# Two projection blocks placed later in a hand-written order, and the experts' down weights read in one run for each partition

## The reference, cut to what matters

```
h = rmsnorm(x, g_attn);  proj = h @ w_in          # u | q_lat | kv_lat | k_pe | q_mem | 3 gates
c_kv = rmsnorm(kv_lat, g_kvlat)
q = rmsnorm(rmsnorm(q_lat, g_qlat) @ w_uq, g_qn)  # then rotary positions
k, v = keys_values(c_kv @ w_ukv)                  # norm and rotary positions on k
merged = sum_i sigmoid(gate_i) * branch_i         # A: S5, B: MLA, C: memory attention
x = x + merged @ w_out
h = rmsnorm(x, g_ffn)
for e in range(32):                               # 2 experts are chosen for each token
    hid = silu(h @ w_e1[e]) * (h @ w_e3[e])       # 1024 -> 256, two products
    y = y + gate[..., e:e+1] * (hid @ w_e2[e])    # 256 -> 1024
x = x + y
```

## Time and profile before

| | |
|---|---|
| median of 3 runs | 638.8 us (636.69, 638.80, 639.08) |
| the profiled execution's own time | 638.72 us |
| its span, first to last instruction | 636.9 us |
| granted TensorE clock, mean of full speed | 0.992 |
| PE busy | 606.7 us, 95% of the span |
| DVE, ACT, POOL busy | 50%, 29%, 23% |
| moved by DMA | 150.57 MB |
| largest shares of the chain that ended last | PE 89%, DVE 4%, issue 2%, DMA 2% |

### The profile page before, as it was taken

One profiled execution on the slowest core, in us unless ns is written; L12 is line 12 of the kernel. 1 busy time (PEld: TensorE's weight loads), 2 busy tenths in 40 slices (PEclk: granted clock), 3 DMA queues, 4 the chain that ended last, 5 costly groups with the idle time before them and its releaser, 6 DMA issues.

```text
span 636.9 us, 10034 instructions
## 1 busy us (share of the span) xinstructions
PE 606.7 (95%) x3742; PEld 378.3 (59%) x3742; DVE 321.1 (50%) x858; ACT 184.0 (29%) x579; POOL 149.1 (23%) x341
## 2 busy tenths in 40 slices
PE   8999999999999999999999999999999999887994
PEld 7888867777456667666677767854434443333441
DVE  3343947757883589772043222685524425425133
ACT  5534224532478445432100101212121121210100
POOL 1596627733584524510000000000000000000000
PEclk9999999999899999999999999999999999999899
DMA  9783553212301343323589990199999999999993
GB/s 302 180 289 108 193 171 100 68 66 84 113 2 33 127 139 100 100 67 100 150 255 395 404 388 20 38 369 415 417 416 415 418 415 417 418 416 418 412 408 112
DMA packets 61683, 150.57 MB, mean 236 GB/s; under 512 B 12352, under 2 KB 40448, under 8 KB 53696
## 3 DMA queue, kind: packets, MB, share of 16 engines
q1 hardware_dynamic: 61632, 149.89, 63.5%
HBM read 147.12 MB, written 2.76 MB: 235 GB/s over the span
## 4 chain that ended last, share of the span: by engine, by line
PE 89%; DVE 4%; issue 2%; DMA 2%; ACT 1%; SPq 0%; DVEq 0%
PE PS L832 28%; PE PS L842 21%; PE PS L1216 9%; PE PS L1113 7%; PE PS L1255 5%; PE PS L1245 5%; PE PS L958 2%; PE PS L915 2%; DVE X L2117 2%; PE PS L983 2%; PE PS L825 1%; PE PS L1166 1%; PE PS L1025 1%; DMA W<-in_w_in 1%; PE PS L966 1%
## 5 line engine op out<-in xcount | busy, mean ns | idle before, releaser
L832 PE MATMUL PS<-hT,W 128*128 128x320 f32 x416 | 117.2, 436 | 0.0
L832 PEld LDWEIGHTS PS<-hT,W 128*128 128x128 f32 x416 | 77.5, 190 | 33.4 <-issue 3.8
L1216 PE MATMUL PS<-E,xT 128*32 128x256 f32 (+1 forms) x1088 | 60.1, 374 | 8.5 <-issue 8.1
L1216 PEld LDWEIGHTS PS<-E,xT 128*32 128x32 f32 x1088 | 37.5, 112 | 35.5 <-issue 20.2
L2191 POOL TENSOR_SCALAR means<-sums 128x4 f32<-128x4 f32 (+3 forms) x35 | 7.6, 217 | 188.0 <-ACT junk L1358 187.1
L1113 PE MATMUL PS<-h,S 128*128 128x512 f32 (+1 forms) x96 | 48.2, 625 | 0.7 <-DVE S L1974 0.7
L1255 PE MATMUL PS<-yb,WG 128*128 128x512 f32 (+1 forms) x96 | 40.9, 622 | 4.0 <-DVE X L2117 3.1
L842 PE MATMUL PS<-W,hT 128*128 128x256 f32 (+5 forms) x256 | 41.7, 353 | 0.0
L2117 DVE TENSOR_TENSOR X<-X,PS 128x512 f32<-128x512 f32 (+1 forms) x48 | 32.8, 686 | 8.3 <-PE PS L1255 6.7
L842 PEld LDWEIGHTS PS<-W,hT 128*128 128x128 f32 (+1 forms) x256 | 31.5, 163 | 8.4 <-issue 1.3
L842 PE MATMUL PS<-W,mergedT 128*128 128x384 f32 (+3 forms) x192 | 35.7, 381 | 0.0
(11 more groups left out here) (313 smaller groups left out, 976.9 us busy)
## 6 DMA issues: line engine op xcount, KB each, us to landing
E<-in_w_e SPq DMA_DIRECT2D x93, 1024.0 KB, 21.3
W<-in_w_in SPq DMA_DIRECT2D x7, 1536.0 KB, 7.2
W<-in_w_in SPq DMA_DIRECT2D x7, 1024.0 KB, 8.6
W<-in_w_mem_kv SPq DMA_DIRECT2D x4, 1024.0 KB, 6.2
W<-in_w_glu SPq DMA_DIRECT2D x4, 768.0 KB, 7.7
W<-in_w_out SPq DMA_DIRECT2D x2, 1536.0 KB, 15.6
X<-in_x_prompt SPq DMA_DIRECT2D x4, 512.0 KB, 4.6
W<-in_w_o_mem SPq DMA_DIRECT2D x1, 1536.0 KB, 6.6
```

Of the source, the lines that this page charges most:

```text
L832: ins = mm(out[:, 0:TOK], w[:, k, cols:cols + 128], rhs[:, k, :], start=(k == 0), stop=(k == kt - 1))
L1216: ins = mm(PS[r:r + B, 2 + par, 128 * which.start:128 * which.stop], xT[:, k, place_ + B * n:place_ + B * n + B], E13[slot][:, which, k, 1 ...
```

## The change

Two edits, independent of each other. In `middle()`, the last `gateC` step (`gateC` 7) is put in after the `qlT` and `ckT` steps in place of before them, and the last `outC` step (`outC` 7) after `kqT` 15 in place of before it. The source of the down weights is viewed with two neighbouring rows of `w_e2` in one partition (`(p j)` for `(j p)`), so each partition reads 8 KB in one run. For the products to fit, half j of the up products takes every second column of the weights (`j::2`) and no longer 128 columns in a row.

```
-    fill(KD)
-    fills = [("outC", d) for d in range(KD)]
+    while len(fills) > 1:
+        fill()
     for t in range(NT):
         put("qlT", t)
     for j in range(len(KEYS)):
         put("ckT", j)
+    fill(KD)
+    fills = [("outC", d) for d in range(KD)]
     for n in range(len(KQ_UNITS) + KQ_LAG):
...
-        if n in (4, 7, 10, 13, 15, 17, 18, 19):
+        if n in (4, 7, 10, 13, 15, 17, 18):
             fill()
...
-        e2_src = a["w_e2"][0].rearrange("e (j p) n -> p e j n", p=128)
+        e2_src = a["w_e2"][0].rearrange("e (p j) n -> p e j n", j=2)
...
-                                 E13[slot][:, which, k, 128 * j:128 * j + 128], start=(k == 0), stop=(k == KD - 1))
+                                 E13[slot][:, which, k, j::2], start=(k == 0), stop=(k == KD - 1))
```

## The result

The changed kernel took 641.72 us (median of 6 runs, 640.38 to 643.11), the kernel before 638.01 us (6 runs, 636.36 to 639.08). The ratio is 1.0063, 95% interval 1.0045 to 1.0081: **+4.0 us**. The profiled execution took 643.11 us, its span is 641.3 us, its mean granted clock 0.987.

The account below looks back on a forecast made before the run. PE's work was taken to bound the kernel up to the experts, weight delivery from there. 638.72 + 3.9 (4.3 + 0.2 - 0.55) - 3.0 gave 639.6 us; forecast's own range 637.8 to 641.5, overall range 635.2 to 643.0.

Parts of the forecast that it names:

- price of `j::2`: Experts' up products: reading every second float32 was taken as 0; bounds 0 and 26 us for 15 pairs.
- edit 1a: `gateC` 7 behind the transposes: uncovered work starts `kq` 0 at 170.8 in place of 166.50, +4.3 us.
- edit 2: Experts' down weights in 8 KB runs: 0.12 us less for each of 25 down experts, -3.0 us.
- rivals 3 and 4: Rival 3: 8 KB rows no faster, 642.6 us, chance 0.12. Rival 4: low clock lasts longer, 642 us, chance 0.10.
- I take 0.2 more than before: PE's low clock around `gateC` 7 and turn 8: costs 0.2 us more than before, bounds 0 and 3.3.
- Edit 1b: `outC` 7 behind `kqT` 15: covers PE's 0.56 us wait for ACT's copy at 221.74 us, -0.55 us.
- Rival 1: Up products: the stepped moving operand is read slower, up to 661 us, deciding from 0.35 us a pair; chance 0.07.
- Rival 2: Ahead of `kq` 0: moving `gateC` 7 costs nothing if ACT copies `qlT` before about 160; 632.8 to 635.2 us, chance 0.11.
- The side effects: After `gateC` 7's move: later `outC0` load, turn 8's norms and POOL's tables stay hidden, cost nothing.
- The reading of the strip: Queue's GB/s: 408 to 418 without a gap from slice 27 (430 us), far less before that.

Follow-up runs that it names:

- edit 1a alone: Only `gateC` 7 moved behind the `qlT` and `ckT` steps, against the kernel before: 643.34 us, ratio 1.0093, +5.9 us.
- the changed kernel again: The changed kernel, unaltered, run and profiled a second time, against the kernel before: 641.59 us (2 runs), ratio 1.0057.
- strided operand alone: Only the up products' operand takes every second column, down weights loaded as in the kernel before: 638.60 us, ratio 1.0011, +0.7 us.
- 8 KB rows alone: Only the down weights in one 8 KB run per partition, up products over contiguous columns as in the kernel before: 635.65 us, ratio 0.9974, -1.7 us.
- edit 1b alone: Only `outC` 7 moved behind `kqT` 15, against the kernel before: 637.28 us, ratio 0.9991, -0.6 us, interval holds 0.
- edit 2 alone: Only the 8 KB down rows with up products over every second column, against the kernel before: 635.93 us, ratio 0.9982, -1.15 us.
- step of 4: Up products' operand takes every fourth column over two neighbouring k blocks, loads as in the kernel before: 688.67 us, ratio 1.0789, +50 us.
- the shorter store wait: Kernel before, but ACT's first `qlT` copy waits for four stores, not ten, and SP holds later stores back: 635.50 us, ratio 0.9962, -2.4 us.
- the shorter store wait with edit 1a: The shorter store wait plus `gateC` 7 moved behind the transposes: 641.41 us, ratio 1.0057 to the kernel before, +6.0 us over the shorter store wait.

## Why the prediction was right or wrong

The range (635.2 to 643.0) held the time. Whether the likeliest case, no change within 0.5%, came is not clear: the ratio is 0.63% slower, which is beyond it, but its interval (0.45 to 0.81) begins below 0.5, and 641.7 is under the 642.0 that the prediction gave as the border. It lies just above the forecast's own range, which ended at 641.5. The mechanisms were right but for a small price of `j::2`; two sizes were off, both the same way. The forecast had the change at +0.9 us (639.6 less 638.72) and it is +4.0: edit 1a was 1.4 us worse than said and edit 2 was 1.85 us short. That the range held the time is owed to its width, which was there for rivals 3 and 4.

**Edit 1a, +4.3: right in its steps.** The store landed within 0.1 us of 164.06, `gateC` 7 began at 166.03 (165.8 predicted), and turn 8 came behind it. Counted from the start of `gateC` 6, `kq` 0 starts at 20.84 us where before it was 13.85, 7.0 us later, and without the 2.25 us of the next point 4.75. The same count gives 4.75 for the other two profiles that differ from before by this move up to here (edit 1a alone, the changed kernel again). Of the 0.45 us over the forecast 0.3 are the last transposes, which end later.

**"I take 0.2 more than before": the step that failed in edit 1.** The low clock in `gateC` 7 cost 6.61 - 4.36 = 2.25 us (start to start, against `gateC` 6). `kq` 0 to 4 gave back 10.45 - 8.85 = 1.6 us, so against that one profile the clock cost 0.65. And that profile was not typical. The low clock in `kq` 0 to 4 comes in some executions of the kernel before and not in others:

| kernel | own time of the profiled run, us | `kq` 0 to 4, us |
|---|---|---|
| before | 638.72 | 10.45 |
| strided operand alone | 638.88 | 10.55 |
| 8 KB rows alone | 636.79 | 10.55 |
| edit 1b alone | 635.83 | 8.85 |
| edit 2 alone | 635.15 | 8.85 |
| step of 4 | 686.99 | 8.85 |

Those with 10.5 us stand in the upper half of their kernel's runs, those with 8.85 in the lower. The times of 29 runs of the kernel before fall into two groups too, 17 from 636.10 to 637.51 with a mean granted clock of 0.992 to 0.997, and 12 from 638.09 to 639.08 with 0.990 to 0.993. The distance is what the 1.7 us of the low clock would make; that these groups are that clock is argued from six profiles, not shown for each run. The mean clock of a run can't settle it, because the experts' stage has a second low stretch of some 3.5 us in most profiles, `8 KB rows alone` among them but not `edit 2 alone`. That second one costs nothing that shows: these two stages last 207.0 and 207.1 us. And the profile of the shorter store wait, 636.03 us and sixth of its eight runs, has `kq` 0 to 4 at 8.85 us, so that not every spread of such times comes from this clock.

With the move, all four profiles have the clock low in `gateC` 7 (6.1 to 6.7 us), for 2.7 to 4.3 us of it, which costs 1.7 to 2.25 us each, 2.0 in the mean. If the groups are that clock, the move saves 1.7 us in 12 of 29 runs: 2.0 - 0.7 = 1.3. With 4.75 that makes 6.05; measured 5.9. In kind this was rival 4 (the low clock lasts longer). It put 2 to 3 us on top of the forecast where 1.1 came (1.3 less the 0.2 taken), and its chance of 0.10 was far too low: I had priced three waits of 5.0 us in all as hardly worse than 1.5 us of them.

**Edit 1b, -0.55:** measured -0.6, interval wide, the wait seen to go.

**Edit 2, -3.0: the term that was mis-sized.** The rows in 8 KB are worth -1.7, 0.07 and not 0.12 us for each down expert, because I took the rates of two short windows (423 and 402 GB/s) for those of the two row lengths. Rival 3 (8 KB rows no faster) was nearer in size for the edit as a whole, 0 against -3.0 where -1.15 came, but is refuted in kind: from 445 to 550 us every profile with 4 KB rows has 416 or 417 GB/s and every one with 8 KB rows 420 (the step of 4, where PE is slower than the queue, has 393). The six stages with 4 KB rows, without a dip and without the step of 4, last 208.7 to 209.1 us, the four with 8 KB rows 207.0 to 207.4. The Trainium skill's rule ("DMA: Bandwidth & Descriptors", Specifications: rows from 512 B go at line rate) is thus right to 3% here, by the estimate of 408 against 420 GB/s.

**The price of `j::2`, 0:** it is 0.2 us a pair. It fell between the two bounds of the test that I gave (3.45 to 3.7 us right, over 4 wrong). The 5 us of waits that were to hide extra work hid nearly all of it. What came through is not clear of the noise: the medians say +0.5 us (edit 2 alone against 8 KB rows alone) and +0.7 (the operand alone), the lengths of the same profiles' stages 0.05 and 0.3. Rival 1 (the operand is read slower) needed 0.35 us a pair and got 0.2.

**Rival 2** (the move costs nothing) fell as argued, and the shorter store wait with edit 1a shows that even its condition, a copy by ACT before 160, would not have saved it: there ACT copies the first `qlT` at 157.10, and the move still costs 6.0 us.

**The side effects** of edit 1a (the late `outC0`, turn 8's norms, POOL's tables) cost nothing: 5.3 us late at turn 9, less 0.55 for edit 1b, are 4.75, and 4.4 arrive at the first up product.

**The reading of the strip** was off by a slice and too plain: the steady flow begins with slice 28 (430 us), and slices 22 to 24 already have 395 to 404 GB/s. No term of the sum used it.

In sum: 4.75 + 1.3 for edit 1a, -0.6 for 1b, -1.7 for the rows and +0.5 for the operand make 4.25, measured 4.0.

Left open: what the dip of the queue is, and which event decides whether the low clock comes in one execution of the kernel before, and why a stepped operand takes longer.

## What to carry to other kernels

Work that is moved behind a chain of another engine has to be priced with what it covered there, the idle time that it leaves, and the clock that PE has after such an idle stretch. A rate of the queue is read over many periods of the mix and not from the quickest and slowest few microseconds, which here showed a difference of 21 GB/s where the long windows give 12. Where a wait counts more events than it needs, name the ones it needs: that was worth more here than either planned edit.

## What the runs showed of the hardware that was not expected

- A float32 moving operand (in column groups of 32 rows) with a step of 2 elements takes 5% longer (3.81 to 3.89 us in most pairs of 64 matmuls, against 3.64 to 3.66), with a step of 4 twice as long (7.45 us).
- The weights' queue moves 416 GB/s with a third of the bytes in rows of 4 KB and the rest in rows of 8 KB, and 420 with nearly all in 8 KB; by an estimate from the two, 408 for 4 KB alone.
- The granted clock is low over one stretch in some executions and not in others behind the same instructions and the same waits (0.77 to 0.79 and 0.73 to 0.74 us), which is 1.6 to 1.7 us of 638; it was seen in profiles of kernels that are alike up to there, three with it and three without.
- The weights' queue fell to 352 GB/s for 5 us in one execution of a kernel and stayed at 428 in another.
